# The delta core's inverse on 32x32 blocks, with the full-size matmuls put piece by piece between its steps

## What is computed

```python
decay = jnp.exp(jnp.where(causal, gc[..., :, None] - gc[..., None, :], -jnp.inf))
kb = k * beta[..., None]
lower = jnp.where(strict, jnp.einsum('nhcid,nhcjd->nhcij', kb, k) * decay, 0.0)
rhs = jnp.concatenate([v * beta[..., None], kb * jnp.exp(gc)[..., None]], axis=-1)
uw = lax.linalg.triangular_solve(lower, rhs, left_side=True, lower=True, unit_diagonal=True)
u, w = uw[..., :dv], uw[..., dv:]
qk = jnp.einsum('nhcid,nhcjd->nhcij', q, k) * decay

def step(state, inp):
    u_c, w_c, qk_c, qg_c, kd_c, a_c = inp
    v_new = u_c - jnp.einsum('nhik,nhkv->nhiv', w_c, state)
    o = jnp.einsum('nhik,nhkv->nhiv', qg_c, state) + jnp.einsum('nhij,nhjv->nhiv', qk_c, v_new)
    state = state * a_c[..., None, None] + jnp.einsum('nhjk,nhjv->nhkv', kd_c, v_new)
    return state, o
```

## Time and profile before

| | us |
|---|---|
| median of three runs | 3025.43 |
| the profiled execution's own time | 3023.46 |
| span of its trace | 3021.6 |
| PE busy (share of the span) | 2895.5 (96%) |
| POOL busy | 1550.6 (51%) |
| DVE busy | 1268.4 (42%) |
| ACT busy | 1132.0 (37%) |
| the eight units of the delta core | 278.2 |

### The profile page before, as it was taken

The page is one execution under the profiler, slowest core; times in us unless marked ns, Lnnn a source line. Parts: engine busy times, 40 slices in busy tenths (PEclk is TensorE's granted clock), DMA queues, the critical chain, the costliest instruction groups (busy, mean ns, idle before and its releaser), DMA issues.

```text
span 3021.6 us, 52364 instructions
## 1 busy us (share of the span) xinstructions
PE 2895.5 (96%) x21538; PEld 2515.4 (83%) x21538; DVE 1268.4 (42%) x2575; ACT 1132.0 (37%) x1726; POOL 1550.6 (51%) x1243
## 2 busy tenths in 40 slices
PE   6999999999999999999999998899999999999998
PEld 4788777878897778887788876799988999888998
DVE  3221247755554421233212366423446552456552
ACT  2212124333333322213112145433455664465663
POOL 2344353422124434444444443688856688556786
PEclk8999999999999999999999999999999999999999
DMA  6533252210003334343333440254543455343453
GB/s 269 178 105 139 99 203 94 88 57 2 3 3 154 112 103 140 108 191 128 106 136 118 156 155 29 98 178 169 185 166 112 153 170 191 128 166 112 156 174 129
DMA packets 58914, 389.97 MB, mean 129 GB/s; under 512 B 6480, under 2 KB 7760, under 8 KB 21360
## 3 DMA queue, kind: packets, MB, share of 16 engines
q1 hardware_dynamic: 48896, 317.87, 30.6%
q10 hardware_dynamic: 9648, 68.34, 6.0%
q0 software_dynamic: 192, 1.25, 0.1%
HBM read 386.39 MB, written 1.05 MB: 128 GB/s over the span
## 4 chain that ended last, share of the span: by engine, by line
PE 69%; POOL 16%; issue 8%; DVE 4%; ACT 2%; DMA 0%; POOLq 0%; ACTq 0%; DVEq 0%
PE bank L693 18%; PE bank L694 18%; PE bank L695 18%; POOL ring_lo L2858 16%; PE bank L727 2%; PE bank L1367 1%; PE bank L1054 1%; PE bank L1089 1%; PE bank L1101 1%; DVE core L2763 1%; PE bank L1062 0%; DVE core L2707 0%; POOL core L2931 0%; PE bank L1387 0%; PE bank L1065 0%
## 5 line engine op out<-in xcount | busy, mean ns | idle before, releaser
L2858 POOL TENSOR_TENSOR ring_lo<-ring,w_hi 128x512 fp32r<-128x512 f32 (+1 forms) x832 | 1059.5, 1305 | 1033.9 <-ACT w_hi L1529 1033.7
L695 PE MATMUL bank<-h_hi,ring_lo 128*128 128x256 f32 (+1 forms) x3256 | 1076.9, 331 | 0.0
L693 PE MATMUL bank<-h_hi,w_hi 128*128 128x512 f32 (+1 forms) x2384 | 839.1, 352 | 30.1 <-POOL ring_lo L2858 21.3
L694 PE MATMUL bank<-h_lo,w_hi 128*128 128x512 f32 (+1 forms) x2448 | 846.0, 346 | 0.0
L695 PEld LDWEIGHTS bank<-h_hi,ring_lo 128*128 128x128 f32 x3256 | 622.8, 191 | 57.3 <-issue 0.3
L1529 ACT ACTIVATE w_hi<-ring 128x2048 fp32r<-128x2048 f32 (+2 forms) x226 | 395.2, 1750 | 466.9 <-PE bank L695 375.1
L693 PEld LDWEIGHTS bank<-h_hi,w_hi 128*128 128x128 f32 x2384 | 454.3, 191 | 111.1 <-issue 28.4
L694 PEld LDWEIGHTS bank<-h_lo,w_hi 128*128 128x128 f32 x2448 | 467.3, 191 | 52.7
L695 PE MATMUL bank<-hid_r,ring_lo 128*128 128x256 f32 (+1 forms) x1088 | 364.1, 335 | 0.0
L2248 DVE SCALAR_TENSOR_TENSOR core<-core,bank 128x512 f32<-128x512 f32 (+1 forms) x88 | 54.6, 621 | 634.2 <-ACT core L1628 634.2
L693 PE MATMUL bank<-hid_r,w_hi 128*128 128x512 f32 (+1 forms) x808 | 285.8, 354 | 2.3 <-POOL ring_lo L2858 2.3
(11 more groups left out here) (440 smaller groups left out, 4220.7 us busy)
## 6 DMA issues: line engine op xcount, KB each, us to landing
ring<-w SPq DMA_DIRECT2D x88, 1024.0 KB, 4.9
ring<-up SPq DMA_DIRECT2D x48, 1024.0 KB, 4.8
ring<-w SPq DMA_DIRECT2D x64, 704.0 KB, 4.1
zbuf<-ada_later ACTq DMA_DIRECT2D x33, 1024.0 KB, 7.0
ring<-down SPq DMA_DIRECT2D x32, 768.0 KB, 4.3
core<-ada_later ACTq DMA_DIRECT2D x16, 1024.0 KB, 6.9
ring<-dn_in SPq DMA_DIRECT2D x16, 1024.0 KB, 4.8
ring<-mla_in SPq DMA_DIRECT2D x16, 1024.0 KB, 4.9
```

The source lines that it names most:

```text
L693: pe.matmul(out, a[0], b[0], start=start, stop=False)
L694: pe.matmul(out, a[0], b[1], start=False, stop=False)
L695: return pe.matmul(out, a[1], b[0], start=False, stop=stop)
L2858: ins = pool.tensor_tensor(like(ring_lo[:, r, a:b], part), like(ring[:, r, a:b], part), part.bitcast(F32), ALU.subtract)
```

## The change

All five engines' orders in the delta core change. The blocks of the inverse are kept as four blocks of 32 rows (BLOCKS, BK = 32), and X and XT have 32 columns for each head instead of 64. So all products of squares, fourths, diagonals, seen_rows and updates are 32x32, four of them for each head instead of two. The first two levels (8 to 16, 16 to 32) are done in this form. The third level (32 to 64) becomes pair_rows, pair_take, pair_update, pair_seeing and pair_seen, each on the blocks that it concerns. seen_half (ACT, two copies of 32 rows) and pair_seeing (DVE) put the 64-row form XS together that join_rows reads. XTF is now filled by one GpSimd product with a mask (spread), by pair_seen (DVE, two copies) and by inverse_join. The memset of XTF at the start becomes one of XS. turned_blocks now makes both transposes' homes on PE (the second product is with the identity as weights), and one DVE product, near_blocks, takes YL and NT together from PSUM. masked(0) and the old near_blocks by halves go.

In PE's order the two directions of key_turn, key_state, decay_row, value_turn, key_key and key_query are no longer neighbours: one piece of four matmuls stands after each step of the inverse. head_sums are cut in pieces of two heads. The half of outputs that multiplies the state becomes state_queries, ahead of outputs, so that it doesn't wait for values_out. On DVE decay_gap is cut in pieces of two heads, residual is put between the steps, lower moves behind pair_seen, and query_decay of the next unit stands behind take_out and take_state when the unit is even (ahead of them when it is odd). On ACT and POOL the order follows.

```diff
+BK = 32
 def turned_blocks(U, s):
-    for hd in range(QUAD):
-        for r in HALVES:
-            mm = pe.matmul(small4(s, C0)[r, hd, :], q[f"LT{U % 2}"][r, hd, r], identc[r, :], start=True, stop=True)
+    for hd in range(QUAD):
+        for r in BLOCKS:
+            pe.matmul(small2(s, C0)[r, hd, :], q[f"LT{U % 2}"][r, hd, r], identc[r, :], start=True, stop=True)
+    for hd in range(QUAD):
+        for r in BLOCKS:
+            mm = pe.matmul(small2(s, C0, 1)[r, hd, :], identc[r, :], q[f"LT{U % 2}"][r, hd, r], start=True, stop=True)
 def squares(U, s):
-    pe.wait_ge(dn["ym"][s], 5 * U + 2)
+    pe.wait_ge(dn["ym"][s], 4 * U + 1)
-        for r in HALVES:
-            pe.matmul(small4(s, C1, 0)[r, hd, :], q["NT"][r, hd, :], q["YL"][r, hd, :], start=True, stop=True)
+        for r in BLOCKS:
+            pe.matmul(small2(s, C1, 0)[r, hd, :], q["NT"][r, hd, :], q["YL"][r, hd, :], start=True, stop=True)
...
+def pair_rows(U, s):
+    pe.wait_ge(dn["xu"][s], 5 * U + 3)
+    for hd in range(QUAD):
+        for seen, seeing in zip(NEAR_SEEN[s], NEAR_SEEING[s]):
+            mm = pe.matmul(small2(s, C0)[seeing, hd, :], q[f"LT{U % 2}"][seen, hd, seeing], q["X"][seen, hd, :],
+                           start=True, stop=True)
+def pair_update(U, s):
+    pe.wait_ge(dn["ym"][s], 4 * U + 4)
+    seeing = NEAR_SEEING[s][s]
+    for hd in range(QUAD):
+        mm = pe.matmul(small2(s, C1, 0)[seeing, hd, :], q["XT"][seeing, hd, :], q["YL"][seeing, hd, :], start=True, stop=True)
+    mm.then_inc(dn["z"][s], 1)
+    for hd in range(QUAD):
+        for seen, seeing in zip(NEAR_SEEN[s], NEAR_SEEING[s]):
+            mm = pe.matmul(small2(s, C1, 1)[seen, hd, :], q["YL"][seeing, hd, :], q["XT"][seeing, hd, :],
+                           start=True, stop=True)
 def join_rows(U, s):
-    pe.wait_ge(dn["xu"][s], 4 * U + 4)
+    pe.wait_ge(dn["xu"][s], 5 * U + 4)
+    pe.wait_ge(dn["inv"][s], 6 * U + 3)
 def join(U, s):
-    pe.wait_ge(dn["inv"][s], 5 * U + 3)
+    pe.wait_ge(dn["inv"][s], 6 * U + 4)
+    pe.wait_ge(dn["qdm"][s], 3 * U + 3)
+    pe.wait_ge(dn["xu"][s], 5 * U + 5)
```

PE's order of a unit, after (s is the last argument; "more" means that a next unit exists, "fresh" that it also needs new values and keys, "sums" that head_sums of the last unit are due):

```diff
+turned_blocks(U, 0); turned_blocks(U, 1); key_turn(U, 0)
+squares(U, 0); squares(U, 1); key_turn(U, 1)
+fourths(U, 0); fourths(U, 1); key_state(U, 0)
+diagonals(U, 0); diagonals(U, 1); key_state(U, 1)
+seen_rows(U, 1, 0); seen_rows(U, 1, 1); decay_row(U + 1, 0)            # more
+updates(U, 1, 0); updates(U, 1, 1); decay_row(U + 1, 1)                # more
+seen_rows(U, 2, 0); seen_rows(U, 2, 1); value_turn(U + 1, 0)           # fresh; sums: head_sums(U - 1, 0, (0, 1))
+updates(U, 2, 0); updates(U, 2, 1); value_turn(U + 1, 1)               # fresh; sums: head_sums(U - 1, 0, (2, 3))
+pair_rows(U, 0); pair_rows(U, 1); key_key(U + 1, 0)                    # fresh; sums: head_sums(U - 1, 1, (0, 1))
+pair_update(U, 0); pair_update(U, 1); key_key(U + 1, 1)                # fresh; sums: head_sums(U - 1, 1, (2, 3))
+join_rows(U, 0); join_rows(U, 1); key_query(U + 1, 0)                  # fresh
+join(U, 0); join(U, 1); key_query(U + 1, 1)                            # fresh
+new_values(U, 0); new_values(U, 1); state_queries(U, 0); state_queries(U, 1)
+outputs(U, 0); next_state(U, 0); outputs(U, 1); next_state(U, 1)
```

The new functions on the other engines:

```diff
+def near_blocks(U, s):                                   # DVE
+    dve.wait_ge(dn["y"][s], 7 * U + 1)
+    dve.tensor_tensor(quad[s]["YN"], turned, edge(s), ALU.mult).then_inc(dn["ym"][s], 1)
+def pair_take(U, s):                                     # DVE
+    dve.wait_ge(dn["y"][s], 7 * U + 5)
+    dve.tensor_scalar(quad[s]["YL"], small2(s, C0), -1.0, None, ALU.mult).then_inc(dn["ym"][s], 1)
+def pair_seeing(U, s):                                   # DVE
+    dve.wait_ge(dn["z"][s], 7 * U + 5)
+    dve.tensor_copy(q["XS"][r, :, t], small2(s, C1, 0)[r, :, :]).then_inc(dn["xu"][s], 1)
+def pair_seen(U, s):                                     # DVE
+    dve.wait_ge(dn["z"][s], 7 * U + 6)
+    dve.wait_ge(dn["qdm"][s], 3 * U + 3)
+    for seen, seeing in zip(NEAR_SEEN[s], NEAR_SEEING[s]):
+        ins = dve.tensor_copy(q["XTF"][seen, :, seeing], small2(s, C1, 1)[seen, :, :])
+def seen_half(U, s):                                     # ACT
+    act.wait_ge(dn["xu"][s], 5 * U + 3)
+    for r, t in IN_SEEN[s]:
+        ins = act.activation(q["XS"][r, :, t], q["X"][r, :, :], ACT.Copy)
+def spread(U, s):                                        # GpSimd
+    pool.wait_ge(dn["xu"][s], 5 * U + 3)
+    pool.tensor_tensor(q["XTF"]..., q["XT"]..., own_block..., ALU.mult).then_inc(dn["qdm"][s], 1)
```

More of the change, by code:

```diff
@@ L1122, in delta_core @@
                     fresh = more and U % 2 == 1
-                    for s in range(2):
-                        turned_blocks(U, s)
-                    for s in range(2):
-                        key_state(U, s)
-                    for s in range(2):
-                        squares(U, s)
-                    for s in range(2):
-                        key_turn(U, s)
-                    for s in range(2):
-                        fourths(U, s)
-                    if more:
-                        for s in range(2):
-                            decay_row(U + 1, s)
@@ L1151, in delta_core @@
-                    for s in range(2):
-                        join_rows(U, s)
-                    if fresh:
-                        for s in range(2):
-                            key_query(U + 1, s)
-                    for s in range(2):
-                        join(U, s)
-                    for s in range(2):
-                        new_values(U, s)
+                    sums = U % 2 == 0 and U > 0
+                    turned_blocks(U, 0)
+                    turned_blocks(U, 1)
+                    key_turn(U, 0)
@@ new lines, in delta_core @@
+                    squares(U, 0)
+                    squares(U, 1)
+                    key_turn(U, 1)
+                    fourths(U, 0)
+                    fourths(U, 1)
+                    key_state(U, 0)
+                    diagonals(U, 0)
+                    diagonals(U, 1)
+                    key_state(U, 1)
+                    seen_rows(U, 1, 0)
+                    seen_rows(U, 1, 1)
+                    if more:
+                        decay_row(U + 1, 0)
+                    updates(U, 1, 0)
@@ new lines, in delta_core @@
+                    updates(U, 1, 1)
+                    if more:
+                        decay_row(U + 1, 1)
+                    seen_rows(U, 2, 0)
+                    seen_rows(U, 2, 1)
+                    if fresh:
+                        value_turn(U + 1, 0)
+                    if sums:
+                        head_sums(U - 1, 0, (0, 1))
+                    updates(U, 2, 0)
+                    updates(U, 2, 1)
+                    if fresh:
+                        value_turn(U + 1, 1)
@@ new lines, in delta_core @@
+                    if sums:
+                        head_sums(U - 1, 0, (2, 3))
+                    pair_rows(U, 0)
+                    pair_rows(U, 1)
+                    if fresh:
+                        key_key(U + 1, 0)
+                    if sums:
+                        head_sums(U - 1, 1, (0, 1))
+                    pair_update(U, 0)
+                    pair_update(U, 1)
+                    if fresh:
+                        key_key(U + 1, 1)
+                    if sums:
+                        head_sums(U - 1, 1, (2, 3))
@@ L1160, in delta_core @@
+                    join_rows(U, 0)
+                    join_rows(U, 1)
+                    if fresh:
+                        key_query(U + 1, 0)
+                    join(U, 0)
+                    join(U, 1)
+                    if fresh:
+                        key_query(U + 1, 1)
+                    new_values(U, 0)
+                    new_values(U, 1)
+                    state_queries(U, 0)
+                    state_queries(U, 1)
                     for s in range(2):
@@ L2789, in delta_core_dve @@
                 for s in range(2):
-                    dve.memset(quad[s]["XTF"], 0.0)
-                for part in (decay_gap, lower, near_blocks, query_decay):
+                    dve.memset(quad[s]["XS"], 0.0)
+                for part in (decay_gap, lower, query_decay):
                     for s in range(2):
@@ L2821, in delta_core_dve @@
                         take_state(U, s)
+                    if more and U % 2 == 0:
+                        for s in range(2):
+                            query_decay(U + 1, s)
                 for s in range(2):
```

274 lines of the change are left out of this document (149 added, 125 removed).

## The result

The changed kernel takes 3071.36 us (median, 3067.05 to 3079.54) against 3024.07 for the kernel before (3022.66 to 3027.24). The ratio is 1.0162, with a 95% interval of 1.0149 to 1.0174. The change costs 47 us where 37 were to be gained. The profiled execution took 3069.43 us (span 3067.5), 46.0 more than that of before.

A forecast was written before the change was run, and what follows sets the result against it. TensorE was taken as the bound in every unit of the delta core. Terms of 88.3 + 105.3 + 19.7 + 15 + 12 gave 240.3 us against 278.2, so -38 us; forecast 2988 us, range 2978 to 3000.

The forecast's parts named there:

- Can the sequencer feed it?: Instruction feed of TensorE's small blocks: eight record pairs pass in about 0.1 us, so 16 matmuls take 0.2 to 0.4.
- the floor on the pace: Rival for the 32x32 groups: records start no closer than 29 ns on average, group 0.93 us, total 3160; chance 0.05.
- Clock, taken as 0 with bounds of 12: TensorE's lower clock in the core: costs 12 us before and after, change 0, bounds -12 and +12.
- Full-size work, 105.3: The core's full-size matmuls, such as key_turn and outputs: 56 pairs of 1.78 us and three head_sums, 105 us before and after.
- Group time, 0.27: Inverse steps on TensorE: 16 matmuls of 32x32 take 0.27 us, four diagonal blocks running at once.
- two at a time: Rival for the inverse: diagonal 32x32 blocks run only in pairs, group 0.51 us, total 3045, slower; chance 0.11.
- Changes of tile size, +9.2: TensorE switching between full-size and small blocks in the core: 78 changes become 146, 0.135 us each, +9.2 us.
- Idle time, 15 us: TensorE's waits in the core: 15 us after against some 16 before, -1 us; 6.7 of it at near_blocks ahead of squares.
- Inverse, -45.8: Inverse steps in the eight units: 16.8 us a unit falls to 11.0, gain 5.7 a unit, -45.8 us in all.

The follow-up runs named there:

- run 5: The kernel before with 1024 extra 32x32 matmuls ahead of TensorE's delta core, twice, as hardware loops of 16 and 64 passes: 3073.48 us, 52.6 more.
- run 2: The changed kernel without the 32x32 products of heads 2 and 3 in units 1, 3, 5 and 7: 3009.62 us, 62 less than the changed kernel.
- run 4: The changed kernel with 64 extra 128x512 matmuls, one ahead of each piece of full-size work in the core: 3091.05 us, 20 more than the changed kernel.
- run 1: The kernel before with a straight-line bench of extra 32x32, 64x64 and 128x128 matmuls, without waits, ahead of TensorE's delta core: 3122.48 us, 99.5 more.

## Why the prediction was wrong

*The step that failed* is the sentence that begins "Can the sequencer feed it?". From two wait records 0.1 us apart I worked out 0.2 to 0.4 us for a group's 64 instructions, 3 to 6 ns each. The row was misread as well. Between the two waits lie four transposes, and a transpose leaves one matmul record and one weight load, not two of each: decay_row's seven units with two directions and four heads are 56 calls and 56 records.

```profile
L946 PE MATMUL bank<-con,tok 128*128 128x128 f32 x56 | 7.6, 278 | 0.0
```

So it was four pairs, eight instructions, and the row gives 0.4 to 0.8 us for a group, at or over the 0.41 at which the whole gain was gone. What TensorE and its sequencer can do is still as fast as I said: the loop of run 5 reaches 5.8 ns, and groups of 0.27 us run where their instructions are there. But these were eight instructions that were there already, and the question was one of 2200 in a row. The rate at which new ones arrive, 14 ns, is three times too slow for groups of 0.27 us. No row of before shows that rate as a wait, because the 64x64 steps use an instruction each 14.7 ns (0.47 us for 32), just slow enough. The page of before did hold the count (128 packets, 2.10 MB on q8), and I hadn't asked how far apart packets come in the densest stretch.

*The rival nearest to it* was the floor on the pace, with a chance of 0.05. I dismissed it because L1072, with half the records, takes as long as L1017. That shows what the array does, and says nothing on the supply. Its figure of 29 ns per record was, over long runs, nearly the right one: 256 instructions in 3.6 us are 28 ns per matmul record. Its time, 3160, was too high because it charged every group that pace in full. Packets keep coming while full-size pieces run, and part of a burst can be there when it begins.

*The sum, term by term.* I had 240.3 us for the core and it took 323.5, 83 more. Waiting for instructions is 53.6 of them, a term that the sum didn't have. The other idle time is 4 us and not 15, so 11 less. Busy time is 265.5 instead of 225.3, so 40 more, and that is the clock:
- *Clock, taken as 0 with bounds of 12.* The core had 164 us at 1.2 GHz instead of 27. The windows of those 164 us, added up, say what TensorE did in them:

```profile
sum 163.84, PE 142.10 PEld 130.70 DVE 59.53 ACT 49.64 POOL 22.40; mean PE 10.93 PEld 10.05 DVE 4.58 ACT 3.82 POOL 1.72
```

  So 142.1 us of busy time and only 22 of the 58 us of idle time lay there. Work at 1.2 GHz took 1.6 times as long (a group, 0.43 after 0.27) to 1.84 times (16 records of 128x128, 3.78 after 2.05), so the clock cost some 53 to 65 us, an estimate. That leaves 200 to 212 us of work at the full clock, where I had 213.3. The dips go where the gaps go (run 2) and are gone when the same small matmuls run without stalls (run 5), so they follow from the stalls here. I had bounded the clock apart from everything else, as if what made TensorE idle couldn't also slow it.
- *Full-size work, 105.3:* 14 us too much, in both kernels alike. 16 of the 56 pairs are transposes (decay_row, value_turn, key_turn), which leave 8 records a pair and not 16, so 0.89 us and not 1.78. The difference of 38 doesn't contain it. But that my sum left 16 us of idle time in the kernel before, where the trace has 17.1, was luck: with the right count it leaves 30, and no run says what the other 13 are.
- *Group time, 0.27:* right, 0.27 to 0.28. Four diagonal blocks do run at once. At the lower clock a group takes 0.43. The rival "two at a time" falls. The Trainium skill (TensorEngine Tiling (Array Packing), "Gotcha 1: PSUM Pressure") says that different row tiles can't write the same PSUM bank at once; the four of L1026 write one bank and run in 0.28 us, so here the measurement decides against it. Likewise 32 matmul records in 0.27 us are 8.4 ns each, below the 25 ns that the Trainium skill (TensorE: Matmul & The Clock Gate, "Wait — 56ns, not 53.3ns?") gives as the least distance.
- *Changes of tile size, +9.2:* not contradicted. A piece of four transposes (L1016) ahead of squares takes 0.58 us from its start to the next, 0.44 for its records and 0.14 for the change.
- *Idle time, 15 us:* too high. near_blocks was late where I put it, ahead of squares, but three times and 3.2 us in all, at most 1.5 at once, where I had 6.7. TensorE comes later to that place by its own gaps, which covers DVE. new_values doesn't wait any more, as forecast.
- *Inverse, -45.8:* real as far as the estimate above goes, and never received. With 27 us at 1.2 GHz taken off in the same way the kernel before has some 250 us of work, the changed one 200 to 212, so 38 to 50 less where the inverse and the changes of tile size were to give 36.6. Less work in the engine didn't shorten the time, since the work wasn't what the time was made of any more.

*What bounds the kernel:* TensorE, as I said, but "TensorE" was two bounds, its array and its instruction supply. The change relieved the first and nearly doubled the load on the second (1184 to 1328 instructions a unit before, 2144 to 2288 after). At 14 ns, 2144 instructions alone are 30 us; the forecast for such a unit was 24. Over the eight units, 17,800 instructions, it is 249 us, 9 more than my sum. This division would have shown the forecast to be out of reach, but not that the change loses: 249 is still less than 278. I put the rest down to bursts that find little held ready, and to the clock.

*What stays open.* How the 83 us part exactly into gaps and clock, since a slower clock uses instructions more slowly and so shortens the gaps. How many packets are held ahead: run 4, the units' lengths (37 to 44 us for 30 to 32 us of supply) and the 196 records ahead of the first gap of run 1 say one or two, but no run was made to count them. And why packets come no closer than 3.4 us: no run changes it.

## What to carry to other kernels

Before splitting matmuls into smaller ones, divide the forecast time of the densest stretch by its number of instructions (four for each float32 matmul, two for each transpose): under about 14 ns each, in straight-line code, the number of instructions sets the time, and merging them is worth more than shrinking their work. The stretch must be that of the small blocks and not a whole unit: unit 1 had 33 us of forecast for 2288 instructions, 14.4 ns each, and took 41.0. Take a rate from a stretch as long as the one it is used for, never from a short burst. Where a change has two parts, as an order and a form, cost and try them apart: here the order was worth keeping (0.9978, with one more move 0.9951) and the form wasn't.

## What the runs showed of the hardware

- Instructions arrive in packets of 16 KB, 256 each, every 3.4 to 3.8 us while TensorE waits for them (once 4.0), at either clock. The gaps reach 2.1 us in the changed kernel. The Trainium skill (Runtime: NRT & Kernel Launch, "Instruction fetch mechanics") has the same blocks of 256 but calls the fetch hidden, since the sequencer is slower than the refill. By the traces it isn't hidden for TensorE below 14 ns an instruction.
- A hardware loop of 256 instructions a pass runs without any such packet, at 5.8 ns each, and a pass costs about 0.2 us.
- Four 32x32 matmuls on diagonal blocks run at once, 16 of them (64 instructions) in 0.27 us at 2.4 GHz and 0.43 at 1.2.
- A float32 transpose leaves one matmul record and one weight load, a float32 matmul two of each (L946, 64 records for 64 calls; L1017, 16 for 8).
- The lower clock follows the stalls: 1024 matmuls of 32x32 had a granted clock of 0.55 in straight line with stalls, and 0.93 and 1.00 as loops without. In the core it was 164 us of 323 at 1.2 GHz with 58 us of idle time, 7 of 259 with 5.
